# Joint attentions: sample scores in two halves a unit, and the order of their side work

## The reference

```python
def _diff_attend(q, k, v, qpos, kpos, lam):
    scores = jnp.einsum('bthed,bshed->bhets', q2, k2).astype(jnp.float32) * SCALE
    mask = (kpos // CHUNK)[None, :] <= (qpos // CHUNK)[:, None]
    p = jax.nn.softmax(jnp.where(mask, scores, NEG_INF), axis=-1)
    attn = p[:, :, 0] - lam * p[:, :, 1]
    return jnp.einsum('bhts,bshd->bthd', attn.astype(v.dtype), v)

def _fox_attend(q, k, v, cq, ck, qpos, kpos):
    scores = jnp.einsum('bthd,bshd->bhts', q, k).astype(jnp.float32) * SCALE
    scores = scores + jnp.moveaxis(cq, 1, 2)[..., :, None] - jnp.moveaxis(ck, 1, 2)[..., None, :]
    p = jax.nn.softmax(jnp.where(kpos[None, :] <= qpos[:, None], scores, NEG_INF), axis=-1)
    return jnp.einsum('bhts,bshd->bthd', p.astype(v.dtype), v)
```

## Time and profile before

| what | value |
|---|---|
| median of three runs | 3878.53 us |
| the profiled execution | 3852.3 us, its span 3850.6 us |
| mean granted clock of TensorE | 0.943 of full |
| busy share of the span: TensorE, VectorE, ScalarE, GpSimd | 90%, 42%, 28%, 7% |
| HBM read and written | 409 MB and 84 MB |
| first joint attention, about | 432 to 784 us |
| second joint attention, about | 2148 to 2848 us |

### The profile page before, as it was taken

How to read it: one execution, slowest core, us unless ns; L and a number is a source line. 1 busy time by engine, 2 the same in 40 slices (tenths; PEclk the granted TensorE clock), 3 DMA queues, 4 the chain that set the end, 5 groups by cost and what they waited for, 6 DMA issues and landing times. The chain is left out here.

```text
span 3850.6 us, 63167 instructions
## 1 busy us (share of the span) xinstructions
PE 3470.9 (90%) x25160; PEld 3003.2 (78%) x25160; DVE 1623.8 (42%) x2919; ACT 1068.1 (28%) x2130; POOL 256.6 (7%) x338
## 2 busy tenths in 40 slices
PE   8988588877999999996999689989979899999997
PEld 7866366666999999995899566666657799999997
DVE  5317466544334233336211265565543333333334
ACT  4215244333121111113221143344333211111211
POOL 2310000023000000004000000000003100000003
PEclk9999599988999999998999789999989899999999
DMA  5447598634111111103553888988842211111102
GB/s 171 120 138 162 143 284 271 222 140 131 44 33 35 52 44 33 54 22 124 144 173 105 213 242 255 276 257 256 276 156 104 77 54 44 33 54 37 40 22 104
DMA packets 421232, 495.33 MB, mean 129 GB/s; under 512 B 97968, under 2 KB 273616, under 8 KB 420880
## 3 DMA queue, kind: packets, MB, share of 16 engines
q1 hardware_dynamic: 421024, 492.45, 42.5%
HBM read 409.20 MB, written 84.10 MB: 128 GB/s over the span
## 5 line engine op out<-in xcount | busy, mean ns | idle before, releaser
L2426 DVE TENSOR_TENSOR f_gated<-f_gated,f_up 128x384 f32<-128x384 f32 x132 | 73.2, 555 | 741.2 <-ACT f_gated L2359 741.2
L2525 PE MATMUL f_gate<-m_ht_hi,f_w_hi 128*128 128x384 f32 x1056 | 355.3, 336 | 25.8 <-DVE f_w_lo L2418 25.8
L2450 DVE TENSOR_TENSOR f_y<-f_y,f_down 128x512 f32<-128x512 f32 x396 | 269.7, 687 | 229.4 <-PE f_down L2538 229.3
L2525 PE MATMUL f_gate<-m_ht_hi,f_w_lo 128*128 128x384 f32 x1056 | 354.9, 336 | 0.0
L2525 PE MATMUL f_gate<-m_ht_lo,f_w_hi 128*128 128x384 f32 x1056 | 354.8, 336 | 0.0
L2525 PE MATMUL f_up<-m_ht_hi,f_w_lo 128*128 128x384 f32 x1056 | 352.7, 334 | 0.0
L2525 PE MATMUL f_up<-m_ht_lo,f_w_hi 128*128 128x384 f32 x1056 | 352.7, 334 | 0.0
L2525 PE MATMUL f_up<-m_ht_hi,f_w_hi 128*128 128x384 f32 x1056 | 352.7, 334 | 0.0
L2538 PE MATMUL f_down<-f_wo_hi,f_act_hi 128*128 128x512 f32 x792 | 312.7, 395 | 10.6 <-DVE f_y L2450 9.3
L2538 PE MATMUL f_down<-f_wo_hi,f_act_lo 128*128 128x512 f32 x792 | 309.2, 390 | 0.0
L2538 PE MATMUL f_down<-f_wo_lo,f_act_hi 128*128 128x512 f32 x792 | 309.1, 390 | 0.0
(11 more groups left out here) (378 smaller groups left out, 6817.3 us busy)
## 6 DMA issues: line engine op xcount, KB each, us to landing
jc_kc<-in_cache_c_k SPq DMA_DIRECT2D x64, 1024.0 KB, 5.9
jc_vc<-in_cache_c_v SPq DMA_DIRECT2D x64, 1024.0 KB, 11.5
f_raw<-in_w_ffn_in SPq DMA_DIRECT2D x88, 512.0 KB
jb_kc<-in_cache_b_k SPq DMA_DIRECT2D x32, 1024.0 KB, 8.5
jb_vc<-in_cache_b_v SPq DMA_DIRECT2D x32, 1024.0 KB, 11.1
f_raw_o<-in_w_ffn_out SPq DMA_DIRECT2D x22, 1024.0 KB, 6.1
f_raw<-x SPq DMA_DIRECT2D x18, 512.0 KB, 4.1
abp_raw<-in_w_ab_in SPq DMA_DIRECT2D x32, 256.0 KB, 3.0
```

The costliest lines, as they stand in the source:

```text
L2426: dve.tensor_tensor(prod[:, b], silu[:, b], up[:, q, 0:gw], ALU.mult).then_inc(prod_done, 1)
L2450: dve.tensor_tensor(part, part, down[:, half, :], ALU.add).then_inc(added, 1)
L2525: last = pe.matmul(acc[:, q, 0:gw], a[:, s, k, u, :], b[:, k, token], start=(k == 0 and j == 0), stop=(k == KT - 1 and j == 2))
```

## The change

- Sample scores come in two halves of the keys, eight tiles each. The first half is computed in step 4 of the unit, the second in step 0 of the next one; in each, two of the four row groups go ahead of the attend and two behind it, in matmuls of 256 columns. Both results of a half stand in the same two PSUM banks.
- Two key tiles are turned in every step. The query blocks are copied in step 2, the new keys turned in step 3.
- The sample maximum moves to step 1, behind that step's output, the exponential to step 2 and in place (`s_probs` is `s_scores`), the turns of sample probabilities to step 3 (two groups) and step 4 (three), their product with the values to step 6, the scaling and the turn of the output to step 7, behind its attend.
- VectorE copies both groups of step 3 and the second of step 5 out of the ring. `probs` has two buffers instead of three.
- Keys are loaded in eight parts of two tiles. In the second attention values are loaded and outputs stored for two heads at once; in the first the values are loaded once for a pair. SP's order changes with it.
- The scores of the first head no longer wait for the selector, the mask and the last GpSimd clears.
- `project_c` stores the negated decay sums in the order in which the bias rows are read, so that a bias load is rows of 512 neighbours.

```diff
-                    dve.tensor_scalar(sum_s[:], sum_s[:], -1.0, None, ALU.mult).then_inc(sample_done, 1)
+                    dve.tensor_scalar(logf_s[:, 0:PAST].rearrange("p (a t r) -> p a t r", a=4, r=32),
+                                      sum_s[:, 0:PAST].rearrange("p (t a r) -> p a t r", a=4, r=32), -1.0, None,
+                                      ALU.mult).then_inc(sample_done, 1)
+                    dve.tensor_scalar(logf_s[:, PAST:], sum_s[:, PAST:], -1.0, None, ALU.mult).then_inc(sample_done, 1)
...
-    turns_at = ((0, 1, 2), (3, 4, 5), (6, 7, 8), (9, 10, 11), (12, 13), (14, 15), (), ())
-    probs_at = ((), (), (0, 1, 2), (3, 4), (), (), (), ())
+    half = parts * per // 2
+    probs_at = ((), (), (), (0, 1), (2, 3, 4), (), (), ())
+    dve_groups = ((3, 0), (3, 1), (5, 1))
...
-        vp = st.sb("vp", [P, 2, TILES_P, dv])
-        probs, probs_t = st.sb("probs", [P, 3, PROMPT]), st.sb("probs_t", [P, 2, TILES_P, P])
+        vp = st.sb("vp", [P, 2, TILES_P, P])
+        probs, probs_t = st.sb("probs", [P, 2, PROMPT]), st.sb("probs_t", [P, 2, TILES_P, P])
...
-        s_scores, s_probs = st.sb("s_scores", [P, keys]), st.sb("s_probs", [P, keys])
+        s_scores = st.sb("s_scores", [P, keys])
+        s_probs = s_scores
...
             load_qk(0)
             load_v(0)
+            load_keys(0, 0)
+            load_keys(0, 1)
             load_q(0)
-            load_keys(0, 0)
...
+            load_keys(0, 2)
+            load_keys(0, 3)
+            load_qk(1)
+            sp.wait_ge(setup, 12)
+            if not diff:
                 sp.dma_start(later[:], row_mask).then_inc(later_loaded, 16)
...
+            load_bias(0)
+            load_new_keys(0)
+            for x in range(4, k_parts):
+                load_keys(0, x)
...
-                    for x in range(parts):
+                    for x in range(4):
                         load_keys(u + 1, x)
+                if u + 2 < U:
+                    load_qk(u + 2)
+                if u + 1 < U:
+                    load_keys(u + 1, 4)
+                    load_keys(u + 1, 5)
                     load_new_keys(u + 1)
                 load_values(u)
+                if u + 1 < U:
+                    load_keys(u + 1, 6)
+                    load_keys(u + 1, 7)
+                if u % 2 == 1:
+                    if u + 3 < U:
+                        load_v((u + 3) // 2)
+                    store(u // 2)
...
-            def score_group(u, first):
-                if first == 0:
-                    pe.wait_ge(kt_done, parts * per * (u + 1))
-                    if u:
-                        pe.wait_ge(scaled, u)
-                pe.wait_ge(s_copied, 4 * u + first)
+            def score_half(u, x, pair):
+                if pair == 0:
+                    pe.wait_ge(kt_done, 2 * half * u + half * (x + 1))
...
+                    if u and x:
+                        pe.wait_ge(scaled, u)
+                    pe.wait_ge(s_copied, 4 * u + 2 * x)
...
+                            dst = s_ps[Q * c:Q * c + Q, a % 2, half * Q * pair:half * Q * (pair + 1)]
...
-            pe.wait_ge(setup, 12)
-            if not diff:
-                pe.wait_ge(later_loaded, 80)
+            pe.wait_ge(setup, 8)
...
-                        if s == 6:
-                            turn_output(u - 1)
+                    if 1 <= u <= U and s == 0:
+                        score_half(u - 1, 1, 0)
+                    if u < U and s == 4:
...
+                        score_half(u, 0, 0)
                     attend(n)
-                    if 1 <= u <= U and s == 4:
+                    if 1 <= u <= U and s == 0:
+                        score_half(u - 1, 1, 1)
+                    if u < U and s == 4:
+                        score_half(u, 0, 1)
+                    if 1 <= u <= U and s == 6:
                         attend_sample(u - 1)
-                    if u < U and s >= 6:
-                        score_group(u, 2 * (s - 6))
+                    if 1 <= u <= U and s == 7:
+                        turn_output(u - 1)
...
-                    if u < U and s == 0:
-                        blocks(u)
                     maximum(n + 3)
-                    if 1 <= u <= U and s == 5:
+                    if 1 <= u <= U and s == 7:
                         scale_output(u - 1)
                     copy_prompt(dve, "dve", n + 1)
                     if u < U:
-                        for t in turns_at[s][0:2]:
+                        for t in (2 * s, 2 * s + 1):
                             turn_keys(u, t)
-                        if s == 4:
+                        if s == 2:
...
+                            blocks(u)
+                        if s == 3:
                             turn_new(u)
-                    if 1 <= u <= U:
-                        if s == 0:
-                            maximum_sample(u - 1)
-                        if s == 2:
-                            inverse_sample(u - 1)
-                        if s == 6:
-                            copy_out(u - 1)
+                    if 1 <= u <= U and s == 3:
+                        inverse_sample(u - 1)
                     output(n)
-                    if u < U:
-                        for t in turns_at[s][2:]:
-                            turn_keys(u, t)
+                    if 1 <= u <= U and s == 1:
+                        maximum_sample(u - 1)
+                    if 1 <= u <= U and s == 7:
+                        copy_out(u - 1)
```

More of the change, by code:

```diff
@@ L1172, in joint_attention @@
     span = per * P
+    k_parts, k_per = 2 * parts, per // 2
+    k_span = k_per * P
     keys = PAST + FRAMES
@@ L1197, in use_prompt @@
         if n < steps:
-            done = sum(len(g) for g in group_of_step[:n % S])
             for g in range(len(group_of_step[n % S])):
-                use(("p", n, g), "dve" if (done + g) % 4 == 3 else "act")
+                use(("p", n, g), "dve" if (n % S, g) in dve_groups else "act")
     use_prompt(0)
@@ L1231, in joint_attention @@
         o_ps = s_ps[:, 0, 0:P]
-        kc, vc = st.sb("kc", [P, parts, per, width]), st.sb("vc", [P, parts, per, width])
+        kc, vc = st.sb("kc", [P, k_parts, k_per, width]), st.sb("vc", [P, parts, per, width])
         kn, vn = st.sb("kn", [Q, width]), st.sb("vn", [FRAMES, width])
@@ L1380, in _ @@
                     load_bias(u + 1)
-                    for x in range(parts):
+                    for x in range(4):
                         load_keys(u + 1, x)
+                if u + 2 < U:
[3 more added lines that the diff above has]
+                    load_keys(u + 1, 5)
                     load_new_keys(u + 1)
                 load_values(u)
-                if u + 2 < U:
-                    load_qk(u + 2)
-                    load_v(u + 2)
-                store(u)
+                if u + 1 < U:
[5 more added lines that the diff above has]
+                    store(u // 2)
             for e in range(2):
-                n_stored = sum(h % 2 == e for h in range(U) if not (diff and h % 2 == 0))
+                n_stored = sum((1 if diff else p % 2) == e for p in range(U // 2))
                 if n_stored:
@@ L1473, in turn @@
                     for x in range(a, b):
-                        last = pe.transpose(slot[:, (x - a) * P:(x - a + 1) * P], probs[:, n % 3, x * P:(x + 1) * P], ident[:])
+                        last = pe.transpose(slot[:, (x - a) * P:(x - a + 1) * P], probs[:, n % 2, x * P:(x + 1) * P], ident[:])
                     last.then_inc(turn_done, 1)
@@ L1495, in score_group @@
                         pe.wait_ge(scaled, u)
-                pe.wait_ge(s_copied, 4 * u + first)
+                    pe.wait_ge(s_copied, 4 * u + 2 * x)
+                else:
+                    pe.wait_ge(s_done, 4 * u + 2 * x + 1)
                 for step in range(4 if diff else 5):
                     for c in range(4):
-                        for a in (first, first + 1):
+                        for a in (2 * pair, 2 * pair + 1):
                             rows_a, hb = slice(Q * a, Q * a + Q), 4 * c + step
@@ L1501, in score_group @@
                             if step < 4:
-                                weights, moving = q_blocks[rows_a, hb // 2, hb % 2], kt[rows_a, :, Q * hb:Q * hb + Q]
+                                weights = q_blocks[rows_a, hb // 2, hb % 2]
+                                moving = kt[rows_a, half * x:half * x + half, Q * hb:Q * hb + Q]
                             else:
                                 weights = select[rows_a, Q * c:Q * c + Q]
-                                moving = bias[rows_a, u % 2, 0:bank].rearrange("p (t r) -> p t r", r=Q)
@@ L1506, in score_group @@
-                            last = pe.matmul(s_ps[Q * c:Q * c + Q, a % 2].rearrange("p (t r) -> p t r", r=Q), weights, moving,
+                                moving = bias[rows_a, u % 2, half * Q * x:half * Q * (x + 1)].rearrange(
+                                    "p (t r) -> p t r", r=Q)
```

(14 more changed lines are left out.)

152 lines of the change are left out of this document (71 added, 81 removed).

## The result

The changed kernel takes 3936.9 us in the median (3931.3 to 3943.7, four runs), the kernel before 3870.6 beside it (3862.6 to 3883.3): 1.0169 of before, 95% interval 1.013 to 1.0208. The profiled execution has a span of 3929.5 us against 3850.6. The prediction was 3855, and its range ended at 3892: it is wrong in sign.

A forecast was written before the change was run, and what follows sets the result against it. TensorE in its program order was taken as the bound. Units -12 us (22 at -0.55), start and tail -13, projection +1 summed to -24: 3828 us profiled, 3855 in the median, range 3808 to 3892.

The forecast's parts named there:

- (1): VectorE's wait at L1720, holding up the attend of step 1, goes as blocks are copied at step 2: -3.3 us a unit.
- (2) to (4): TensorE's waits a unit: old ring waits -2.6 us, new wait at step 3 +3.9, ring waits at step 4 +1.1.
- The wait at step 3: The attend of step 3 waits for VectorE's chain of 8.66 us, leaving TensorE idle 3.9 us a unit.
- The ring waits: At step 4 three groups of sample turns follow a two-group turn in the same ring: 1.1 us a unit kept.
- (5): Sample scores as 320 matmuls of 256 columns: streaming time unchanged (taken 0, bounds 0 and +8.6), two more drains +0.35 us a unit.
- (7): DMA loads regrouped: TensorE and VectorE don't wait for DMA, so nothing saved in the units and no loss.
- The clock: TensorE's low clock behind the long wait costs the same 2.0 us a unit as before, bounds 0 and 4.0.
- Rival B: Clock stays low through step 4, over the two score groups: +42 us, 3920 us; chance 0.12.
- The bound of 0.88 for the mean clock: Sign of being wrong: mean granted clock in the attention stretches under 0.88 (or above 0.97).
- (8): Second attention starts 11 us earlier; start -17.5 us, tail +4.6, together -13, between -7 and -17.
- Rival D: Unit time equal, early start of the second attention eaten by late keys: -10 to 0 us, 3873 us; chance 0.14.
- Rival C: Half-size score batches take 0.30 us instead of 0.215: +46 us, 3925 us; chance 0.08.

The follow-up runs named there:

- e2: Changed kernel with half as many score matmuls, each of 512 columns reading its 256 twice, row groups 2 and 3 left out; 0.9954 of before.
- e4: Changed kernel with the loads of the prompt's queries and keys issued later in SP's order, same bytes and TensorE instructions; 1.0088 of before.
- e12: Changed kernel with only the prompt's query and key loads cut to 32 columns from the third head on, samples loaded in full; 1.0029 of before.
- e5: Kernel before with VectorE's order alone changed: blocks at step 2, sample maximum behind step 0's output, key tiles spread differently; 0.9955 of before.
- e6: e5 with TensorE starting each attention early, waiting for bias and selector rows only at step 5 of the first unit; 0.994 of before.
- e10: Changed kernel with nearly all key and value loads (second unit on) and prompt query and key loads (third head on) cut; 0.9955 of before.
- e3: Changed kernel in which each key or value part loads only one tile from the second unit on, TensorE's instructions the same; 1.0167 of before.
- e7: e5 with the four bias matmuls of a row group made one with 128 columns of weights; 0.9987 of before.
- e9: e6 with sample turns at steps 3 and 4, what follows one step later, and no key tile at step 0; 0.9954 of before.

## Why the prediction was wrong

**(1) The wait at L1720** went as said; its counterpart waits for nothing. **(2) to (4)** The wait at step 3 came, at 1.8 us instead of 3.9; it stands ahead of the turn of the next tile, which needs a ring slot back from VectorE's copy, and not ahead of the attend. The ring waits were 2.0 us a unit ((19.2 + 6.1 and two smaller ones) / 15) instead of 1.1. Against 3.3 + 2.6 before, the waits that have a semaphore fell by 2.1 us, more than the 0.9 predicted. This part of the working is right in its mechanism and was too gloomy in sum.

**(5) is the step that failed.** It priced the added matmuls by their columns and their issue, and both prices hold: 43 weight loads in 1.02 us are 24 ns each, and a group takes 2.4 us at full clock, against 4.5 for twice the columns. The Trainium skill's 62 ns a matmul (page "TensorE: Matmul & The Clock Gate", section "Wait — 56ns, not 53.3ns?"), which the page gives for hardware decode off, has the direction of the result, but not its mechanism: nothing here runs at that rate. What the step left out is that an instruction must be brought. 320 added records a unit (160 matmuls and their loads) are 1.25 more blocks of 256, run through at a weight load each 24 to 27 ns. Bounds of 0 and +8.6 us stood there, and "the nearer in kind" was taken with nothing in it for supply. The term was put at +0.35; measured, it is 5.5 us a unit of the second attention (46.2 in the change, 40.7 in e2) and 1.5 of the first (39.3 and 37.8). Of the 5.5, 2.2 are standing (29.0 us over the 13 units of the window), the rest mostly clock.

**(7) failed with it.** "TensorE and VectorE don't wait for DMA now, so this saves nothing" is true of data. TensorE did wait for DMA after the change, for its own instructions, and the place of the prompt's loads decided how often (e4, e12).

**The clock** was kept at a cost of 2.0 us a unit with bounds 0 and 4.0. Its mean fell from 0.92 to 0.84, 60 / 15 = 4.0 us a unit more than before, so 6.0 in all with the 2.0 that the prediction took for before. Rival B had nearly the size (+42 us; the medians differ by 66) and the place, low clock over the dense work of step 4, but gave it the wrong cause, the wait at step 3. In e2 that wait is 2.1 us long as well, and the clock stays at 0.91. The bound of 0.88 for the mean clock, named as a sign of being wrong, was passed.

**(8) The start** was right for TensorE, 2158.36 for 2169.46, 11.1 us earlier (9.6 us after its first load, 10 to 11 predicted). The bytes in the queue were over-counted: seven query and key loads are six of 256 KB and one of 8, so 1.5 MB and not 1.75, 6.5 MB in all and not 7.0. Little of the start reached the work: the output of the first step of unit 1 came 9.6 us earlier (2208.7 for 2218.3) and the first sample maximum, which the change puts a step later, 1.9 us (3.0, counted from the stage's first load). The clock was 0.54 over the first 41.6 us, against 0.78 before. The prediction took 17.5 us less 4.6 for it. Against e5, e6 shows the same start giving nothing (0.7 us, in a stage that began 0.9 us earlier). Rival D had the small gain, but from late keys; what the rows show is the clock.

```profile
2158.40:2200.00 41.60, 39.99 (x330) 30.58 (x331) 19.15 (x41) 11.23 (x29) 0.00 (x0) 0.54 1.08 271
```

```profile
2169.50:2211.00 41.50, 36.42 (x333) 26.85 (x341) 22.68 (x49) 14.07 (x35) 0.00 (x0) 0.78 1.06 304
```

**Rival C** (batches that don't halve) predicted nearly the right time, 3925, by a cause that the timeline refutes: they do halve. Without late blocks the change is worth -18 us (e2) and -17 us (e10, which has less traffic as well), near the -24 of the forecast. That the sum comes this near is in part luck: in e2's trace the units give the 12 us that were forecast (4 in the second attention, 8 in the first), though its waits were mis-sized, and the stretch between the attentions, with the start in it, gives 2.5 instead of 13. The loss is a part that was not in the sum.

What stays open: why the prompt's queries and keys hold up a block more than sample keys do, what fills the 1.2 to 2.0 us between a packet's end and TensorE's next instruction, and why some stops are followed by a low clock and others are not.

## What to carry to other kernels

Before splitting matmuls, count instructions: blocks of 256 in a dense run, against the time that the engine takes for them, and look at the queue that brings them. Where TensorE stands on "issue" for over a microsecond inside a group of equal instructions, compare the places with multiples of 256 and look for a packet of instructions 2 to 3 us before it goes on. The cures, by what they gave here: fewer and wider instructions (e2), then bursts of loads moved away from the dense run (e4); the mean DMA share does not show the risk (e3).

## What the hardware showed

- A packet of 256 instructions took 1.1 us with traffic and without. In the median it started 0.7 us after TensorE had entered a block with the DMA share at 0.11 (e10), 3.8 us after in the changed kernel at 0.74, at most 15.5 us after.
- The data queue stands at 104% of 16 engines in the view of the stop. Within the changed kernel's trace, packets started 0.6 us after the entry of a block with the data queue under 20% busy, and 4.1 us after with it over 80%.
- One stop of 2.6 us was followed by 11.8 us at a granted clock of 0.50, over work that filled TensorE completely. Behind the changed kernel's 15 stops the mean over 10 us was 0.67; behind nine stops of 1.0 to 1.6 us in e2, e5, e6, e7 and e9 it was 1.00.
- The kernel before, with a higher mean DMA share (0.84), had no such stop in the second attention, and one of 1.56 us in the first (at 712.1 us, at a block's end too): it stood close to the edge. Its reordered form e9 had four.
